# Head shares, evacuations, key requests and the first pair cycle of each feed-forward layer issued in another order

## Chip, cores and metric

One Trainium2 chip, one core used. The metric is the time on the device in microseconds (us) of one launch; lower is better.

## The reference, cut to what matters

Two layers over 576 tokens (512 of a prompt, 64 of a later request that also has 128 cached keys per head), width 1024, all fp32.

```python
def _diff_attend(q_pos, q, k, v, k_pos, rel_table, lam):
    k2 = k.reshape(k.shape[:3] + (2, DIFF_DIM))
    bias = jnp.moveaxis(_rel_bias(k_pos[None, :] - q_pos[:, None], rel_table), -1, 0)
    logits = jnp.einsum('bqhmd,bkhmd->bmhqk', q, k2).astype(jnp.float32) * DIFF_SCALE + bias
    logits = jnp.where(_chunk_mask(q_pos, k_pos), logits, -jnp.inf)
    p = jax.nn.softmax(logits, axis=-1)
    attn = (p[:, 0] - lam * p[:, 1]).astype(v.dtype)
    return jnp.einsum('bhqk,bkhd->bqhd', attn, v)
# even layer: x += concat(latent attention of 8 heads ("mla"),
#                         _rmsnorm(_diff_attend of 8 heads, g_subln)) @ w_out
# odd layer:  x += attention of 8 heads over the 256 keys that an indexer selects ("dsa") @ w_out
# each layer then: h = rmsnorm(x); x += (silu(h @ w_gate) * (h @ w_up)) @ w_down
```

## The kernel before

**Numbers.** Every fp32 operand of a product is split into a high and a low part, and a product is three matmuls: high by high, low by high, high by low. The split of a weight `RAW` is a rounding copy on ScalarE (`WH`, L1892 in attention, L2181 in the feed-forward part) and a subtraction on VectorE (`WL`, L2407, L2860) or on GpSimd (`WL`, L3170).

**Heads.** The 24 heads (0 to 7 mla, 8 to 15 diff, 16 to 23 dsa) run one after another. The function `attention(h)` stands four times, for TensorE (L1531), ScalarE (L2050), VectorE (L2747) and GpSimd (L3256), and each goes through 8 slots `s`. In slots 0 to 4 TensorE makes the scores of token tile `s` (`head_scores`, L1442 and L1418) and transposes the probabilities of the tile before (`turn_probs`, L1455 to L1458). VectorE and ScalarE do the softmax between: mask and maximum L2659, exponent L2016, reciprocal L2667, scaling L2024 in mla and dsa heads; in diff heads the two maps are mixed by `mix_maps` (VectorE L2677). The transposes are split by L2032 (ScalarE) and L2684 (VectorE, `PTl`) before `weighted_values` (L1467) may use them.

**Shares.** A slot also has a share of a later head's projections. `CHUNKS` says which: in mla heads one whole projection (`q`, `k`, `v` and for even heads `pe`, `ps`), in diff and dsa heads a part of q, k and v. A share is a run of 128x288 matmuls of L1206 into one of the two PSUM pairs ACC0 and ACC1, which `group(..., use=LONG or SHORT)` names in `plan_attention`; VectorE reads it out in `write_projection` (`YQ`, `YK`, `YV`; L2585 in diff and dsa heads), and the values are then split in jobs q, k, v: high parts on ScalarE (L1923), low parts on GpSimd (L3177: `Ql`, `Kl`, `Vl`). Odd heads have in slots 0 to 3, even heads in slots 4 to 7, a tile of the output projection of a finished pair of heads (`wo`, L1206 from MIX), added to X by VectorE (L2423).

**Cached keys.** In slot 4 of heads 8 to 14 GpSimd asks for the next head's cached keys (`load_cached_keys`, DMA of KC, L3242) and then does job v; TensorE transposes KC at the end of the head (L1372).

**Norm of a diff head.** Its sums of squares are ten one-column matmuls (`subnorm_sum`, L1214, into ACC1) in slot 3 of the next head. `b_mean` (VectorE L2435, L2436, L2439) reads them out, ScalarE takes the root (L2048), and L1222 spreads the result.

**Feed-forward part.** Its weights run in seven-product cycles over pairs of tiles (`cycle`, L1586 to L1588). The first two tiles, m = 0 and 1 (`PLAIN` = 2), are made one by one with gate and up products (L1206); VectorE copies the up products from PSUM into U (L2985, L2994), ScalarE makes SG (L2189), and GpSimd multiplies (HF, L3320) and splits (HH, L3322) while VectorE prepares the first cycle: sums of token halves (XD, L2896 to L2903), their low parts (TB, L2909), mixed weights (T and S, L2831 to L2847) and the weights' low parts (L2860). ScalarE copies finished products out of PSUM (TC, L2161).

**Order.** Each engine runs its list as it is written out by these functions. Only counted semaphores tie the engines together, so an instruction that waits holds up all behind it on its engine.

## Time and profile before

| | us |
|---|---|
| median of 3 runs | 1730.51 (1728.37 to 1733.53) |
| the profiled execution | 1732.16 |
| its span, first to last instruction | 1730.3 |
| TensorE busy in the span | 1678.6 (97%) |
| VectorE, ScalarE, GpSimd busy | 1114.3, 803.5, 584.6 |
| mean granted TensorE clock | 0.992 of full speed |

The page of the profile gives for each engine its busy time, then the clock in 40 slices, the chain of work that ended last and the costliest groups. Times of rows are microseconds from the start of the span. `[1.45 <-POOL Ql L3177]` behind a row says that the engine had idled 1.45 us before it and that the last thing it waited for was `Ql` of L3177 on GpSimd (POOL). PE is TensorE, DVE VectorE, ACT ScalarE.

### The profile page before, as it was taken

The page shows a single profiled execution, that of the slowest core. Times are in us where ns is not written, and L with a number is a line of the kernel's source. Part 1 is how long each engine was busy: PE and PEld are TensorE (multiplying, and loading weights), DVE is VectorE, ACT ScalarE, POOL GpSimd, SP SyncE. Part 2 cuts the span into 40 slices and gives each one's busy share as a digit, 9 for nine tenths or more (in the row PEclk, how much of TensorE's full clock was granted, in tenths as well). Part 3 has the DMA queues.
Part 4 walks back from the last instruction along what each step waited for, and adds up shares of the span by engine and source line. Part 5 has one row for each costly group of instructions (what it writes and reads, how often), then busy time and mean ns, then how long its engine had stood idle before and what let it go on. Part 6 is the DMA issues. An engine that isn't in the chain of part 4 may idle for free.

```text
span 1730.3 us, 31752 instructions
## 1 busy us (share of the span) xinstructions
PE 1678.6 (97%) x12337; PEld 1617.3 (93%) x12345; DVE 1114.3 (64%) x2086; ACT 803.5 (46%) x1522; POOL 584.6 (34%) x442
## 2 busy tenths in 40 slices
PE   7999999999999999999999999999999999999998
PEld 6889999889898899999999999899989999999998
DVE  4656655555556698478467679633457974884776
ACT  4355555354545555245335445543456551552453
POOL 3344344355443122012102248474451230121122
PEclk9999999999999999999999999999999999999999
DMA  7221132332233123223323242332322332333231
GB/s 195 61 54 56 52 98 68 85 83 73 73 87 91 49 62 110 86 73 98 110 62 100 55 115 69 97 95 78 94 85 67 86 110 62 98 107 89 74 90 64
DMA packets 252104, 145.45 MB, mean 84 GB/s; under 512 B 21934, under 2 KB 242156, under 8 KB 251956
## 3 DMA queue, kind: packets, MB, share of 16 engines
q1 hardware_dynamic: 247080, 135.41, 27.6%
q0 software_dynamic: 4032, 7.77, 1.7%
q8 instruction: 100, 1.64, 0.4%
q14 instruction: 48, 0.39, 0.1%
q10 hardware_dynamic: 844, 0.24, 0.1%
HBM read 130.69 MB, written 15.32 MB: 84 GB/s over the span
## 4 chain that ended last, share of the span: by engine, by line
PE 82%; DVE 10%; ACT 3%; issue 3%; POOL 1%; DMA 1%; SPq 0%; DVEq 0%; ACTq 0%
PE ACC L1206 39%; PE ACC L1586 7%; PE ACC L1588 7%; PE ACC L1587 7%; PE T L1206 3%; PE ACC L1467 2%; PE S L1442 2%; PE S L1206 2%; DVE SCO L2732 2%; DVE TOP L2729 1%; ACT PR L2016 1%; PE S L1588 1%; PE S L1586 1%; PE S L1587 1%; PE S L1418 1%
## 5 line engine op out<-in xcount | busy, mean ns | idle before, releaser
L1206 PE MATMUL ACC<-XGh,WH 128*128 128x288 f32 x1024 | 233.6, 310 | 7.5 <-DVE YK L2585 2.1
L3170 POOL TENSOR_TENSOR WL<-RAW,WH 128x1024 fp32r<-128x1024 f32 (+3 forms) x84 | 180.4, 2150 | 156.9 <-ACT WH L1892 156.7
L3320 POOL TENSOR_TENSOR HF<-SG,U 128x576 f32<-128x576 f32 x44 | 66.6, 1515 | 477.7 <-ACT SG L2189 412.1
L1206 PE MATMUL ACC<-XGh,WL 128*128 128x288 f32 x1024 | 221.0, 298 | 0.0
L1206 PE MATMUL ACC<-XGl,WH 128*128 128x288 f32 x1024 | 220.6, 297 | 0.0
L1586 PE MATMUL ACC<-TB,WH 128*128 128x288 f32 x640 | 189.9, 297 | 5.1 <-DVE WL L2860 4.5
L1892 ACT ACTIVATE WH<-RAW 128x1024 fp32r<-128x1024 f32 (+3 forms) x159 | 153.1, 971 | 81.7 <-PE ACC L1206 43.7
L1588 PE MATMUL ACC<-TB,WL 128*128 128x288 f32 x640 | 189.4, 296 | 0.0
L1587 PE MATMUL ACC<-TB,WH 128*128 128x288 f32 x640 | 189.1, 296 | 0.0
L1206 PE MATMUL ACC<-HH,WH 128*128 128x288 f32 x1032 | 179.3, 295 | 0.0
L1206 PEld LDWEIGHTS ACC<-XGh,WH 128*128 128x128 f32 x1024 | 163.7, 191 | 14.2 <-DVE YK L2585 2.6
L1206 PEld LDWEIGHTS ACC<-XGh,WL 128*128 128x128 f32 x1024 | 165.9, 190 | 0.0
L1206 PEld LDWEIGHTS ACC<-XGl,WH 128*128 128x128 f32 x1024 | 165.8, 190 | 0.0
L1206 PEld LDWEIGHTS ACC<-HH,WH 128*128 128x128 f32 x1032 | 151.3, 188 | 0.0
L2016 ACT ACTIVATE PR<-SX,STAT 128x128 f32<-128x128 f32 (+4 forms) x160 | 85.7, 536 | 131.2 <-DVE STAT L2659 127.6
L1586 PEld LDWEIGHTS ACC<-TB,WH 128*128 128x128 f32 x640 | 120.8, 189 | 6.6 <-DVE WL L2860 4.9
L2423 DVE TENSOR_TENSOR X<-ACC,X 128x576 f32<-128x576 f32 x89 | 66.7, 752 | 89.1 <-PE ACC L1206 85.2
L2407 DVE TENSOR_TENSOR WL<-RAW,WH 128x1024 fp32r<-128x1024 f32 (+2 forms) x75 | 96.3, 1285 | 41.9 <-ACT WH L1892 41.6
L1588 PEld LDWEIGHTS ACC<-TB,WL 128*128 128x128 f32 x640 | 121.1, 189 | 0.0
L1587 PEld LDWEIGHTS ACC<-TB,WH 128*128 128x128 f32 x640 | 121.0, 189 | 0.0
L3322 POOL TENSOR_TENSOR HH<-HF,HH 128x576 fp32r<-128x576 f32 x44 | 67.8, 1541 | 137.6 <-ACT HH L2198 137.6
L1206 PE MATMUL ACC<-HH,WL 128*128 128x288 f32 x516 | 110.1, 294 | 0.0
(459 smaller groups left out, 4342.3 us busy)
## 6 DMA issues: line engine op xcount, KB each, us to landing
RAW<-in_w_gate_dram SPq DMA_DIRECT2D x44, 512.0 KB, 3.9
RAW<-in_w_up_dram SPq DMA_DIRECT2D x44, 512.0 KB, 4.6
RAW<-in_w_down_dram SPq DMA_DIRECT2D x32, 512.0 KB, 4.1
RAW<-in_w_in_even_dram SPq DMA_DIRECT2D x29, 512.0 KB, 5.1
RAW<-in_w_in_odd_dram SPq DMA_DIRECT2D x28, 512.0 KB, 4.4
RAW<-in_w_out_even_dram SPq DMA_DIRECT2D x16, 512.0 KB, 4.2
RAW<-in_w_down_dram SPq DMA_DIRECT2D x16, 384.0 KB, 3.5
RAW<-in_w_out_odd_dram SPq DMA_DIRECT2D x8, 512.0 KB, 5.0
```

The source lines that it names most:

```text
L1206: ins = pe.matmul(out[0:m, 512 * b:512 * b + width], left, right[:, b * width:(b + 1) * width], start=(first and part == 0), stop=(last an ...
L1442: ins = pe.matmul(out[0:r, 0:w], left, right, start=(i == 0), stop=(i == len(products) - 1))
L1586: pe.matmul(out, hi[:, w], xh, start=first and k == 0, stop=False, skip_group_check=not first)
L1587: pe.matmul(out, hi[:, w], xl, start=False, stop=False, skip_group_check=not first)
L1588: ins = pe.matmul(out, lo[:, w], xh, start=False, stop=k == 3, skip_group_check=not first)
L1892: act.activation(WH[slot][:, 0:n], RAW[slot][:, 0:n], ACT.Copy).then_inc(w_hi, 1)
L2016: act.activation(PR[m][0:r, n % 2, 0:w], SX[m][0:r, 0:w], ACT.Exp, bias=STAT[0:r, n % 2, m:m + 1], scale=-1.0, accum_out=STAT[0:r, n % 2, ...
L2407: dve.tensor_tensor(WL[slot][:, 0:n], RAW[slot][:, 0:n], WH[slot][:, 0:n].bitcast(F32), ALU.subtract).then_inc(w_lo, 1)
L2423: return lambda out: dve.tensor_tensor(two(X[:, m, :]), halves(out), two(X[:, m, :]), ALU.add)
L3170: pool.tensor_tensor(WL[slot][:, 0:n], RAW[slot][:, 0:n], WH[slot][:, 0:n].bitcast(F32), ALU.subtract).then_inc(w_lo_pool, 1)
L3320: pool.tensor_tensor(HF[:, q, :], SG[:, q, :], U[:, q, :], ALU.mult).then_inc(h_out, 1)
L3322: pool.tensor_tensor(HH[:, m, 1, :], HF[:, q, :], HH[:, m, 0, :].bitcast(F32), ALU.subtract).then_inc(h_lo, 1)
```

## The change

It moves instructions and changes no arithmetic.

1. **Head 0.** The q share of head 1 (18 matmuls) goes ahead of the first scores, the k share of head 1 writes ACC1, the q share of head 2 moves from head 1's first slot to head 0's slot 5, and ScalarE does job k of head 1 earlier.
2. **Head 6, slot 5.** VectorE's weight split moves behind the evacuations.
3. **Heads 8 to 13, slot 5.** VectorE writes YK before the low parts of the transposes (`keys_early`).
4. **Heads 8 to 14.** GpSimd asks for the cached keys behind job v.
5. **Head 15.** The sums of squares of head 14 go behind the `wo` tile of slot 3; `b_mean` moves from slot 3 to slot 4; one X evacuation of slot 5 moves ahead of PTl, in head 22 too.
6. **Head 16.** A share of 12 matmuls goes ahead of the scores of slot 3; VectorE writes YK one slot later.
7. **First pair cycle of both layers.** ScalarE copies U instead of VectorE. GpSimd's first product waits until VectorE has made the cycle's token sums. VectorE makes the last token sum and the next cycle's weight split ahead of the mix of S4. ScalarE copies t2 and rounds the token sum ahead of S4.

```diff
+def share(h, s):
+    if (h, s) == (0, 5):
+        return 2, "q", 0, QLT, QLT
+    g = prepared_in(h)
+    if g is None or (h, s) == (1, 0):
+        return None
+    c = chunks(g)[s]
+    return c and (g, *c)
+def share_first(h, s):
+    return (h, s) in ((0, 0), (16, 3))
...
+    SHORT_TOO = (("k", 1), ("q", 2), ("q", 18))
@@ TensorE, attention @@
+                    if share_first(h, s):
+                        prepare(*c[:4])
                     if s < TOK_TILES:
                         head_scores(h, s)
...
-                    if s == 3 and h % 16 and kind_of(h - 1) == "diff" and h % 2:
+                    if s == 3 and h in (9, 11, 13):
                         subnorm_sum(h - 1)
...
                     if out_tile(h, s) and (h, s) != (22, 4):
                         output_tile(*out_tile(h, s))
+                    if (h, s) == (15, 3):
+                        subnorm_sum(14)
@@ ScalarE, attention and first cycle @@
+                    if h == 0 and s == 4:
+                        job("k", g)
...
+                    if not before and not part:
+                        seven_copy("t2", layer, part, c)
+                        token_sum_hi(layer, 3, 1)
                     seven_high("S4", layer, part, c)
-                    seven_copy("t2", layer, part, c)
...
+            def take_plain_up(layer, m):
+                act.wait_ge(acc_done, acc.made("u", layer, m))
+                act.wait_ge(acc_free, acc.made("g", layer, m))
+                act.activation(two(U[:, m, :]), halves(pair(acc.at("u", layer, m))), ACT.Copy).then_inc(acc_free, 1)
@@ VectorE, attention @@
-                return s == 5 and (h in (2, 4, 6) or h == 23)
+                return s == 5 and h in (2, 4, 6, 15, 22, 23)
+            def keys_early(h, s):
+                return s == 5 and kind_of(h) == "diff" and prepared_in(h) is not None
...
-                    if s == (3 if h % 2 else 4) and h % 16 and kind_of(h - 1) == "diff":
+                    if s == (3 if h in (9, 11, 13) else 4) and h % 16 and kind_of(h - 1) == "diff":
                         b_mean(h - 1)
...
-                    if h < HEADS and s:
+                    if h < HEADS and s and (h, s) != (6, 5):
                         begin("slot", h, s - 1)
+                    if (h, s) == (6, 6):
+                        begin("slot", h, s - 2)
@@ VectorE, first cycle @@
+                    if not before and not part:
+                        token_sum(layer, 3)
                     mix("S4", layer, part, c)
+                    if not before and not part:
+                        seven_low("WG", layer, part, c + 1)
                     add_up("c11", layer, part, c)
                     seven_low("A22", layer, part, c)
-                    if not before and not part:
-                        token_sum(layer, 3)
...
-                evacuate(("u", layer, 0), lambda out: dve.tensor_copy(two(U[:, 0, :]), halves(out)))
@@ GpSimd @@
-                    if s == 4 and x is not None and kind_of(h) != "mla" and h != 16:
+                    if s == 4 and h > 16 and x is not None:
                         load_cached_keys(x)
                     if s == v_job_slot(h):
                         job("v", h)
...
+                    if s == 4 and x is not None and kind_of(h) == "diff":
+                        load_cached_keys(x)
...
                         pool.wait_ge(sg_done, made)
+                        if m == 0 and not part:
+                            pool.wait_ge(tb_lo, 4 * layer + 4)
```

GpSimd's list in head 8, before and after (WL is a weight's low part, KC the cached keys of head 9, VF its cached values, Ql, Vl and Kl the low parts of the head's q, v and k):

```order
L3177 TENSOR_TENSOR Ql_97<-YQ,Qh_95 128x576
L3170 TENSOR_TENSOR WL_58<-RAW_52,WH_55 128x1024
L3242 DMA KC<-in_cache_diff_k_dram 128x128
L3177 TENSOR_TENSOR Vl<-VF,Vh 128x768
L3170 TENSOR_TENSOR WL_59<-RAW_53,WH_56 128x1024
```

```order
L3229 TENSOR_TENSOR Ql_97<-YQ,Qh_95 128x576
L3222 TENSOR_TENSOR WL_58<-RAW_52,WH_55 128x1024
L3229 TENSOR_TENSOR Vl<-VF,Vh 128x768
L3294 DMA KC<-in_cache_diff_k_dram 128x128
L3222 TENSOR_TENSOR WL_59<-RAW_53,WH_56 128x1024
```

The request for KC stood ahead of Vl and now stands behind it. The same is so in each of the heads 8 to 14; in heads 8, 11 and 13 a WL follows, in the others Kl.

TensorE's list in slots 3 and 4 of head 15, before and after (L1214 and, after, L1237 are the sums of squares of head 14; the runs from MIX are tiles of the output projection, the second of them m = 4):

```order
L1455 MATMUL T<-IDN,PR_81 128x128 x2
L1214 MATMUL ACC<-ONES,SQ 128x1 x4
L1214 MATMUL ACC<-ONES,SQ 64x1
L1206 MATMUL ACC<-MIXh,WH_55 128x288 x2
L1206 MATMUL ACC<-MIXl,WH_55 128x288 x2
```

```order
L1229 MATMUL ACC<-MIXl,WH_55 128x288 x2
L1229 MATMUL ACC<-MIXh,WL_58 128x288 x2
L1237 MATMUL ACC<-ONES,SQ 128x1 x4
L1237 MATMUL ACC<-ONES,SQ 64x1
L1441 MATMUL S<-Kh,Qh_95 64x192 x2
L1441 MATMUL S<-Kl,Qh_95 64x192 x2
L1441 MATMUL S<-Kh,Ql_97 64x192 x2
L1478 MATMUL T<-IDN,PR_81 128x128 x3
L1229 MATMUL ACC<-MIXh,WH_56 128x288 x2
```

The sums, which write ACC1, stood ahead of the twelve matmuls of tile m = 3 (ACC0) and now stand behind them; the next that writes ACC1 is tile m = 4, the last row.

VectorE's list at the end of the first pair cycle's preparations in layer 0, before and after (TB is the low part of a token sum XD; T and S are mixed weights; the G row is a sum of finished products):

```order
L2994 COPY U<-ACC 128x576
L2843 TENSOR_TENSOR S<-RAW_52,RAW_53 128x512
L2909 TENSOR_TENSOR TB<-XD,TB 128x1152
L2860 TENSOR_TENSOR WL_60<-S,WH_57 128x512
L2847 TENSOR_TENSOR S<-RAW_52,T 128x512
L2872 TENSOR_TENSOR G<-S,TC 128x288
L2860 TENSOR_TENSOR WL_63<-RAW_53,WH_62 128x512
L2903 TENSOR_TENSOR XD<-XF,XD 128x1152
L2860 TENSOR_TENSOR WL_58<-RAW_54,WH_55 128x1024
L2909 TENSOR_TENSOR TB<-XD,TB 128x1152
```

```order
L2893 TENSOR_TENSOR S<-RAW_52,RAW_53 128x512
L2959 TENSOR_TENSOR TB<-XD,TB 128x1152
L2910 TENSOR_TENSOR WL_60<-S,WH_57 128x512
L2953 TENSOR_TENSOR XD<-XF,XD 128x1152
L2897 TENSOR_TENSOR S<-RAW_52,T 128x512
L2910 TENSOR_TENSOR WL_58<-RAW_54,WH_55 128x1024
L2922 TENSOR_TENSOR G<-S,TC 128x288
L2910 TENSOR_TENSOR WL_63<-RAW_53,WH_62 128x512
L2959 TENSOR_TENSOR TB<-XD,TB 128x1152
```

The copy of U is gone, the last XD and the next cycle's 1024-column WL (WL_58) stand ahead of the G sum and of WL_63, which were ahead of them.

## Rows read from the trace of the kernel before

**Rows 1.** Windows: length; busy PE, PEld, DVE, ACT, POOL; clock; DMA share; GB/s.

```profile
88.00:95.00 7.00, 7.00 (x32) 6.06 (x31) 3.68 (x7) 1.31 (x4) 1.33 (x2) 0.53 0.42 84
...
308.00:313.00 5.00, 3.59 (x16) 3.48 (x17) 4.03 (x7) 1.84 (x4) 2.72 (x5) 0.66 0.37 105
...
559.00:563.00 4.00, 4.00 (x25) 3.50 (x24) 3.32 (x13) 2.08 (x6) 0.00 (x0) 0.61 0.51 124
...
1358.00:1362.00 4.00, 4.00 (x22) 4.00 (x22) 3.90 (x5) 1.58 (x2) 0.00 (x0) 0.64 0.82 232
```

**Rows 2.** TensorE's timeline, head 0: start, duration, instruction, idle before.

```profile
87.20 0.30 PE L1442 MATMUL S<-Kh,Qh 128*128 128x128 f32 x1 [1.45 <-POOL Ql L3177]
...
105.15 0.21 PE L1457 MATMUL T<-IDN,PR 64*64 64x64 f32 x1 [1.73 <-ACT PR L2024]
```

**Rows 3.** The timeline of GpSimd, VectorE and TensorE, head 8, slot 4.

```profile
303.42 0.56 POOL L3242 DMA_DIRECT2D KC<-in_cache_diff_k_dram  x1
...
305.80 2.35 POOL L3170 TENSOR_TENSOR WL<-RAW,WH 128x1024 fp32r<-128x1024 f32 x1
...
303.62 4.75 DVE L2677 SCALAR_TENSOR_TENSOR PR<-PR,STAT,PR 64x192 f32<-64x192 f32 x1
...
308.52 0.21 PE L1457 MATMUL T<-IDN,PR 64*64 64x64 f32 x1 [2.08 <-DVE PR L2677]
...
309.69 0.85 PE L1206 MATMUL ACC<-XGh,WH 128*128 128x288 f32 x2 [0.89 <-DVE YK L2585]
```

**Rows 4.** The timeline in head 9; last, the keys' DMA by line.

```profile
325.19 4.78 POOL L3170 TENSOR_TENSOR WL<-RAW,WH 128x1024 fp32r<-128x1024 f32 x2 [10.73 <-ACT WH L1892]
...
326.95 0.76 DVE L2677 SCALAR_TENSOR_TENSOR PR<-PR,STAT,PR 128x128 f32<-128x128 f32 x1
...
350.62 1.85 POOL L3177 TENSOR_TENSOR Vl<-VF,Vh 128x768 fp32r<-128x768 f32 x1 [2.91 <-ACT Vh L1923]
...
353.97 0.27 PE L1372 MATMUL T<-IDN,KC 128*128 128x128 f32 x1
...
DMA to landing us min/median/max: 2.2/3.2/4.3
```

**Rows 5.** The timeline of TensorE in slot 5 of head 10.

```profile
382.67 0.53 PE L1206 MATMUL ACC<-XGh,WH 128*128 128x288 f32 x2 [0.39 <-DVE YK L2585]
```

**Rows 6.** The timeline of VectorE and TensorE in head 15.

```profile
559.45 0.14 DVE L2436 TENSOR_SCALAR RS<-ACC 64x1 f32<-64x1 f32 x1
...
562.90 0.16 DVE L2667 RECIPROCAL STAT<-STAT 64x2 f32<-64x2 f32 x1 [0.31 <-ACT PR L2016]
...
561.13 0.83 PE L1206 MATMUL ACC<-MIXh,WH 128*128 128x288 f32 x2
...
568.68 0.49 PE L1222 MATMUL ACC<-IDN,RS 128*128 128x128 f32 x2 [1.21 <-DVE X L2423]
```

**Rows 7.** The timeline, first pair cycle, layer 0; last row layer 1.

```profile
615.54 2.41 POOL L3320 TENSOR_TENSOR HF<-SG,U 128x576 f32<-128x576 f32 x1 [32.42 <-DVE U L2985]
...
616.57 2.46 DVE L2860 TENSOR_TENSOR WL<-RAW,WH 128x1024 fp32r<-128x1024 f32 x1
...
623.55 1.22 DVE L2860 TENSOR_TENSOR WL<-T,WH 128x1024 fp32r<-128x1024 f32 x1
...
624.69 0.75 DVE L2994 COPY U<-ACC 128x576 f32<-128x576 f32 x1
...
630.39 0.41 ACT L2161 ACTIVATE TC<-ACC 128x288 f32<-128x288 f32 x1
...
630.90 0.37 PE L1586 MATMUL ACC<-TB,WH 128*128 128x288 f32 x1 [2.25 <-DVE WL L2860]
...
1357.26 0.42 PE L1586 MATMUL ACC<-TB,WH 128*128 128x288 f32 x1 [2.26 <-DVE WL L2860]
```

**Rows 8.** The timeline of TensorE in heads 7 and 16.

```profile
247.69 0.53 PE L1206 MATMUL ACC<-XGh,WH 128*128 128x288 f32 x2 [0.67 <-DVE X L2423]
...
1096.62 0.46 PE L1442 MATMUL S<-Kh,Qh 128*128 128x512 f32 x1 [2.33 <-DVE SEL L2739]
```

More of the change, by code:

```diff
@@ L420, in plan_pairs @@
             if this:
-                if c + 1 < n:
+                if c + 1 < n and (before or part):
                     add(seven_lo, "WG", c + 1)
@@ L2218, in cycle @@
                     ahead(layer, part, 1, "P5")
-                if c >= 2 and (before or part):
+                if c >= 2 and (part or c > PLAIN + 1):
                     hidden_hi(layer, part, c - 2)
+                if not part and c == PLAIN + 1:
+                    hidden_hi(layer, part, 0)
                 if this:
@@ L2934, in cycle @@
                 if this:
-                    if c + 1 < n:
+                    if c + 1 == n:
+                        begin("ahead", layer, part, 0)
+                    elif before or part:
                         seven_low("WG", layer, part, c + 1)
-                    else:
-                        begin("ahead", layer, part, 0)
                     if not before and not part:
@@ L2993, in ffn @@
                 seven_low("S12", layer, 0, PLAIN)
-                evacuate(("u", layer, 1), lambda out: dve.tensor_copy(two(U[:, 1, :]), halves(out)))
                 mix("S3", layer, 0, PLAIN)
```

67 lines of the change are left out of this document (39 added, 28 removed).

## The prediction

> **What bounds the kernel now.** I read the busy shares first, then the waits of TensorE summed by line, then the timeline around each long one. TensorE is busy 97% of the span, so the time is its matmuls, its idle gaps, and the stretches in which its clock is low. The change leaves every product in place, so all it can move is the gaps and those stretches. In the windows of [rows 1] the granted clock is 0.53, 0.66, 0.61 and 0.64: each holds a stretch at 1.2 GHz instead of 2.4. Such a stretch began in each case right behind a place where TensorE had idled or had run only one-column matmuls. A stretch costs about (1 − clock) × length: (1 − 0.53) × 7.0 = 3.3 us in head 0, 0.34 × 5 = 1.7 in head 8, 0.39 × 4 = 1.6 in head 15, 0.36 × 4 = 1.4 in layer 1's feed-forward part. So a gap costs its length, and sometimes 1.4 to 3.3 us more. VectorE, at 64%, is far from full over the whole, but where TensorE idles it is nearly always a chain through VectorE, and twice VectorE is itself held up beside GpSimd [rows 3, 7].
>
> **Head 0.** TensorE idles 1.45 us for GpSimd's `Ql` before the first scores, and near the head's end 1.73 us for ScalarE's scaling [rows 2]. The 18 matmuls moved ahead need nothing from `Ql`, so the 1.45 goes and with it, I think, the half-clock stretch behind it, 3.3. The share of head 2, taken ahead of the last tile's transposes, lies on the 1.73. Removable: 1.45 + 3.3 + 1.73 = 6.5. But with TensorE earlier, the chain of softmax steps and of head 1's keys (VectorE, ScalarE, then `Kl` on GpSimd) ends last at the head's end, and it gets only part of this. I take 5.0; bounds 1.5 (the first gap alone) and 6.5.
>
> **Heads 6 and 7.** The 0.67 us wait for X [rows 8] goes when the weight split moves behind the evacuations: +0.65, bounds 0.3 and 0.7.
>
> **Head 8.** GpSimd writes the request for KC at 303.42. VectorE asks for its mix at 303.62 and has it only at 308.37, behind `Vl` and behind the WL that ends at 308.15; TensorE idles 2.08, then 0.89 for YK, then runs at half clock, 1.7 [rows 1, 3]. After the change `Vl` (1.85 us, as in [rows 4]) runs at 303.43 to 305.28, the request follows, and VectorE's mix gets in at the boundary, at about 305.4. YK is written before the low parts. Left is some 0.6 us for YK. Gain 2.08 + 0.89 + 1.7 − 0.6 = 4.1; lower bound 0, should the mix stay shut out until the WL ends as it did before; upper bound 4.7.
>
> A rule bears on this term. In the trace the mix stayed out through two instructions of GpSimd, `Vl` and WL [rows 3]. The Trainium skill, page "SBUF — State Buffer", section "Who interferes with whom", says that whichever of VectorE (with two inputs in SBUF) and GpSimd starts first holds the shared ports for its whole instruction, and the other is blocked until then. By that rule the mix should have come in when `Vl` ended, so the row shows a longer block than the rule has. By the rule this term is 4.1, by the row as a precedent it is 0.
>
> I take 4.1 because in head 9 the mix was asked for inside two WLs that run back to back (325.19 to 329.97) and was done in 0.76 us, at the boundary between them [rows 4].
>
> **Head 9.** The request for KC now goes out when `Vl` ends, at 350.62 + 1.85 = 352.47. It lands 2.2 to 4.3 us after issue, median 3.2, so at 354.7 to 356.8, and TensorE transposes KC at 353.97 [rows 4]. That is a new wait of 0.7 to 2.8 us; I take −1.5, and −3.5 at worst with a half-clock stretch behind a long one. In the other heads 8 to 14 the same timeline shows the transposes over 5 us behind `Vl`, more than the longest landing.
>
> **Heads 10, 12 and 14.** TensorE waits 0.39 us for YK in head 10 [rows 5] and likewise in the other two; YK written before the low parts ends that: 3 × 0.39 = +1.2. Lower bound 0. The price, if the mix fails to get in between the WL and `Vl`, is a rival below.
>
> **Head 15.** The wait of 1.21 us for X goes [rows 6], and part of a wait for the squares, 0.3. But the sums' reader moves behind the reciprocal of slot 4, which starts at 562.90; before, it read at 559.45. Tile m = 4, which writes the same bank, was begun at 561.13 [rows 6] and must now wait until about 562.7 (the reciprocal comes a little sooner, the reads take 0.3). TensorE would idle about 2.0 to 2.5 us, where now a half-clock stretch of 1.6 [rows 1] lies, which I expect to stay in another place. Gain 1.21 + 0.3, loss 1.6 to 2.5 less what of it is regained at the next wait: −0.1, bounds −1.7 and +1.0.
>
> **Head 16.** Twelve matmuls fill none of the 2.33 us before the selection is ready, because they stand behind scores that wait for it [rows 8]; they make the slot's scores later and its end less idle. With a possible new half-clock stretch, +0.2, bounds −1.2 and +1.0.
>
> **Feed-forward part, layer 0.** TensorE idles 2.25 us at 630.90. The row names a WL, but the bank is freed by ScalarE's copy of t2, begun at 630.39, behind a rounding that waits for VectorE's mix [rows 7]. VectorE gets there late: the WL at 616.57 takes 2.46 us against 1.22 for the same shape at 623.55, because GpSimd's HF began before it; two copies of U cost 2 × 0.75 [rows 7]; a token sum's low part is also about 1.2 us longer beside GpSimd. After the change 1.2 + 1.2 + 1.5 = 3.9 us leave VectorE, and t2 is copied ahead of the rounding. Against that ScalarE copies U behind a rounding, which gives the second up product its bank about 0.5 us later. The gap of 2.25 goes, and with it hardly more, since TensorE has no other long gap there: +2.2, bounds 1.0 and 3.0. What is late next is VectorE's weight split for the following cycle, which the change moves ahead.
>
> **Feed-forward part, layer 1.** The same gap, 2.26 [rows 7], and here the half-clock stretch follows, 1.4 [rows 1]: +3.6, bounds 1.5 and 4.8. GpSimd's held products cost nothing: the next user of their buffers is the gate of tile 2, a whole cycle later.
>
> **Sum.** 5.0 + 0.65 + 4.1 − 1.5 + 1.2 − 0.1 + 0.2 + 2.2 + 3.6 = 15.35. The profiled execution took 1732.16 us, so 1716.8 on its scale. The median of the runs is 1.65 lower, 1730.51, which gives 1715.2. I take 1716.
>
> **Rivals.**
> *The gaps are only partly cured.* Where TensorE comes earlier, it next meets the softmax chain, the keys of head 9 and the bank in head 15, each at its worse bound, and head 0 gives 2.5 instead of 5: 1716 + 2.5 + 2.0 + 1.6 = 1722. For it: all these chains run through the same two engines. Against: the gaps before and after are of different lengths, and the chains have slack at most of them. Chance 0.14.
> *The mix stays shut out for one instruction.* In heads 10, 12 and 14 `Vl` now begins straight behind WL, where the request used to stand between. If GpSimd goes on without letting VectorE in, the mix is late by `Vl`'s 1.85 us, 3 × (1.85 + 0.39), and head 8 gives half: 1716 + 6.7 + 2 = 1725. For it: the block in head 8; against: the mix in head 9. Chance 0.09.
> *Slower: shut out as in head 8.* If every mix asked for beside back-to-back work of GpSimd is held until that work ends, each of the five heads 10 to 14 costs what head 8 cost, 2.08 + 0.89 + 1.7 = 4.7. Head 8 and heads 10, 12 and 14 lose their gains, 4.1 and 1.2: 1716 + 5 × 4.7 + 5.3 = 1745. It decides from the point where GpSimd's next instruction is taken before VectorE's waiting one in at least four of the five. Against it: [rows 4]. Chance 0.04.
> *It doesn't do what it says.* The gaps are there for another reason (the clock drops whatever stands before the scores of head 0, t2's copy is late for another wait), and the gains are eaten: 1729. Chance 0.04.
> The forecast has the remaining 0.69.
>
> **Range and chances.** From the bounds of the unknown costs, the worse ends that may fall together (head 0 at 1.5, head 8 at 0) give 1716 + 3.5 + 4.1 = 1723.6, and the first two rivals reach to 1725; I close at 1726. The better ends (head 0 6.5, both feed-forward parts, head 15 +1.0, head 9 −0.7) sum to 1716 − 1.5 − 2.0 − 1.1 − 0.8 = 1710.6, and what overlaps the half-clock stretches leave open is some 2 us more: 1708. A measurement of this kernel can tell about 0.3%, 5.2 us, from no change: faster means below 1725.3. Faster 0.86, within 0.10, slower 0.04.
>
> **What would show it.** Head 0: no idle before L1442's first scores and a clock near 1 there. Head 8: VectorE's mix done by 306 instead of 308.4, and the clock of 308 to 313 near 1. Head 9: a wait of TensorE for the DMA of KC of 1 to 2 us. Head 15: a wait of tile m = 4 for RS of 2 us or more. Both feed-forward parts: the wait before the seventh product gone, HF begun only after the fourth token sum, and the 1024-column WL at 1.2 us. The prediction is wrong if the mixes of heads 10, 12 and 14 take over 3 us, if gaps gone in one place stand a few us further on with their length, or if new half-clock stretches appear behind the new waits.

## The result

| | median, us | runs | ratio to the kernel before, 95% interval |
|---|---|---|---|
| before | 1729.68 | 4 (1728.37 to 1733.53) | |
| changed | 1715.65 | 4 (1713.06 to 1716.73) | 0.9912 (0.9895 to 0.9929) |

The change makes the kernel 0.9% faster. The profiled execution of the changed kernel took 1716.73 us, its span is 1714.6 (before 1732.16 and 1730.3). The forecast was 1716, in a range of 1708 to 1726. So the total came out, but as will be seen two of its terms were wrong, others made up for them, and 0.69 us of the traced difference arose before any part of the change.

**Where the time went.** TensorE makes the same 12337 matmuls in both kernels, nearly in the same order. So the n-th matmul of one trace can be laid beside the n-th of the other, and the difference of their start times, read at places that no part of the change moves, gives the gain up to that place. The step between two such places is the gain of the stage between them. Each trace is one execution: over the twelve other traces of the experiments below and of a repeat, a step whose instructions are the changed kernel's came out again within 0.06 us in head 0, 0.02 in head 8, some 0.3 in each feed-forward part, but 1.4 to 1.5 in heads 15 and 16. The first step, in which nothing was changed, lies between -0.66 and -1.95 over all of them, so it varies by 1.3 us with the same instructions and is not shown to come from the change.

| stage (read at, us of before) | difference after it | step | forecast |
|---|---|---|---|
| start (59.9) | -0.69 | -0.69 | |
| head 0 (150.0) | -6.28 | -5.59 | -5.0 |
| heads 6 and 7 (260.0) | -7.13 | -0.85 | -0.65 |
| head 8 (329.9) | -11.64 | -4.51 | -4.1 |
| head 9 (370.1) | -10.87 | +0.77 | +1.5 |
| heads 10 to 14 (550.0) | -12.34 | -1.47 | -1.2 |
| head 15 and the end of the layer's attention (592.0) | -11.04 | +1.30 | +0.1 |
| feed-forward part, layer 0 (700.0) | -13.61 | -2.57 | -2.2 |
| up to head 16 (1080.1) | -13.80 | -0.19 | |
| head 16 (1199.9) | -12.59 | +1.21 | -0.2 |
| feed-forward part, layer 1 (1400.1) | -15.68 | -3.09 | -3.6 |
| last matmul (1722.9) | -15.70 | -0.02 | |

The table of windows of the changed kernel (length; busy time and count of PE, PEld, DVE, ACT, POOL; TensorE's granted clock; DMA share; GB/s) covers the places of [rows 1]:

```profile
80.00:90.00 10.00, 9.74 (x70) 8.39 (x69) 6.09 (x13) 4.98 (x9) 2.92 (x2) 1.00 0.07 13
...
296.00:302.00 6.00, 6.00 (x47) 5.77 (x46) 5.61 (x8) 3.31 (x7) 5.98 (x5) 1.00 0.36 98
...
550.00:554.00 4.00, 3.48 (x15) 3.46 (x16) 0.81 (x5) 3.63 (x5) 2.72 (x2) 0.57 0.00 0
...
1090.00:1096.00 6.00, 5.55 (x23) 5.27 (x24) 2.10 (x8) 2.65 (x6) 5.02 (x8) 0.50 0.25 61
...
1343.00:1347.00 4.00, 4.00 (x33) 4.00 (x32) 4.00 (x6) 0.44 (x2) 1.43 (x1) 1.00 0.87 251
```

Head 0 is the first of these rows, head 8 the second, then head 15, head 16 and layer 1's first pair cycle. The clock is 1.00 in head 0, head 8 and layer 1's first pair cycle, where it was 0.53, 0.66 and 0.64. In head 15 it is as low as before, and head 16 has 0.50.

The timeline of TensorE (start, duration, instruction, idle time before it and what ended that) shows both gaps of [rows 2] gone, only one wait of 0.84 us being left, then the last transposes and the v share of head 8 without the waits of [rows 3], the new wait of head 9, and the new wait of head 15:

```profile
98.50 0.63 PE L1478 MATMUL T<-IDN,PR 128*128 128x128 f32 x4 [0.84 <-ACT PR L2051]
...
299.25 0.24 PE L1480 MATMUL T<-IDN,PR 64*64 64x64 f32 x1
...
299.48 0.53 PE L1229 MATMUL ACC<-XGh,WH 128*128 128x288 f32 x2
...
343.04 0.30 PE L1395 MATMUL T<-IDN,KC 128*128 128x128 f32 x1 [0.56 <-DMA KC<-in_cache_diff_k_dram]
...
550.52 0.85 PE L1229 MATMUL ACC<-MIXh,WH 128*128 128x288 f32 x2 [2.95 <-DVE RS L2478]
```

In head 8 GpSimd now begins Vl before it writes the request for the keys, and VectorE's mix, asked for inside Vl, ends with it (296.48 + 1.88 = 298.36; Vl ends at 298.15). In head 10 the mix gets in between WL and Vl (367.67 + 1.12 = 368.79; the WL ends at 368.58), as the row of head 9 in [rows 4] had it:

```profile
296.30 1.85 POOL L3229 TENSOR_TENSOR Vl<-VF,Vh 128x768 fp32r<-128x768 f32 x1
...
296.48 1.88 DVE L2719 SCALAR_TENSOR_TENSOR PR<-PR,STAT,PR 64x192 f32<-64x192 f32 x1
...
368.54 1.93 POOL L3229 TENSOR_TENSOR Vl<-VF,Vh 128x768 fp32r<-128x768 f32 x1
...
367.67 1.12 DVE L2719 SCALAR_TENSOR_TENSOR PR<-PR,STAT,PR 64x192 f32<-64x192 f32 x1
```

In layer 0's first pair cycle ScalarE copies t2 from 616.05 to 616.46, 1 us before the seventh product begins at 617.44, VectorE's split of the next cycle's weight takes 1.22 us and ends at 618.0, 1.0 us before its matmul of 619.03, and GpSimd's first product comes at 620.37, behind all of this. TensorE has no gap there, where [rows 7] had 2.25 us:

```profile
616.05 0.41 ACT L2190 ACTIVATE TC<-ACC 128x288 f32<-128x288 f32 x1 [0.47 <-PE ACC L1615]
...
616.78 1.22 DVE L2910 TENSOR_TENSOR WL<-RAW,WH 128x1024 fp32r<-128x1024 f32 x1
...
620.37 1.43 POOL L3377 TENSOR_TENSOR HF<-SG,U 128x576 f32<-128x576 f32 x1 [48.31 <-DVE TB L2959]
```

### The profile page after: what moved, and what is told of

The parts are those of the page before. It is cut to its first block, busy times and chain, and to the rows that moved or that the text cites. A ratio compares the mean times of both kernels' runs of the same rounds, so it can differ in the third digit from the quotient of the medians.

```text
span 1714.6 us, 31759 instructions
## 1 busy us (share of the span) xinstructions
PE 1672.7 (98%) x12337; PEld 1612.3 (94%) x12345; DVE 1107.5 (65%) x2082; ACT 805.2 (47%) x1526; POOL 581.1 (34%) x442
## 3 DMA queue, kind: packets, MB, share of 16 engines
q8 instruction: 100, 1.64, 0.4%
## 4 chain that ended last, share of the span: by engine, by line
PE 81%; DVE 11%; ACT 4%; issue 2%; POOL 1%; DMA 1%; ACTq 0%; DVEq 0%
PE ACC L1229 40%; PE ACC L1613 7%; PE ACC L1615 7%; PE ACC L1614 7%; PE T L1229 3%; PE ACC L1490 2%; PE S L1229 2%; PE S L1465 2%; DVE SCO L2774 2%; ACT PR L2043 1%; DVE TOP L2771 1%; PE S L1615 1%; PE S L1613 1%; PE S L1614 1%; PE T L1478 1%
```

## The experiments

Each kernel below is the changed kernel with the edit shown, and the traces are compared by the table's method. The theory was that of the prediction: a gap of TensorE costs its length and sometimes a stretch at 1.2 GHz behind it, and the gaps come from late chains, twice through a collision of VectorE and GpSimd. Its rivals stand with each run. Each of the ten experiments was run once, and single times of one kernel differ by some 3 us, so what is read from them is the trace.

### Head 0: which of the two moves

```diff
 def share_first(h, s):
-    return (h, s) in ((0, 0), (16, 3))
+    return (h, s) == (16, 3)
```

> The changed kernel with one thing undone: in head 0 the scores of tile 0 come before the q share of head 1 again. Theory (the idle time starts the half-clock stretch): TensorE idles 1.4 us for Ql before the first scores again, the clock then is at half for some 7 us (a window of 7 us behind it shows 0.5 to 0.6), and against the changed kernel TensorE is 1.4 + 3.3 = 4.7 us late by the k and v share, of which up to 1 us is taken back at the next wait for probabilities: 3.5 to 4.7 us in all. Rival (the slow stretch came from the small transposes there, not from the gap): 1.4 us and the clock stays near 1.

The time was 1718.83 us. The wait for Ql is back to the hundredth, with a slow stretch behind it:

```profile
86.00 0.30 PE L1465 MATMUL S<-Kh,Qh 128*128 128x128 f32 x1 [1.45 <-POOL Ql L3229]
...
88.00:95.00 7.00, 7.00 (x42) 7.00 (x41) 3.70 (x10) 2.30 (x6) 1.50 (x1) 0.76 0.40 84
```

The gap gives 1.45 and the clock (1 - 0.76) x 7 = 1.7. Behind them TensorE is 2.9 us later than in the changed kernel, and 0.7 of these are regained at a later wait for probabilities; head 0's step is -3.35 instead of -5.59, so the share costs 2.2 us where it stood before. That the slow stretch belongs to the scores placed first, with their wait, is shown: it is there in the two traces that have this order, and none of the twelve others has one in head 0. Its price isn't fixed: 1.7 us here, 3.3 in the kernel before [rows 1] for the same 1.45 us of idle time. The expectation, 3.5 to 4.7, was too high by this.

```diff
 def share(h, s):
-    if (h, s) == (0, 5):
-        return 2, "q", 0, QLT, QLT
     g = prepared_in(h)
-    if g is None or (h, s) == (1, 0):
+    if g is None:
...
-    SHORT_TOO = (("k", 1), ("q", 2), ("q", 18))
+    SHORT_TOO = (("k", 1), ("q", 18))
```

> The changed kernel with the q share of head 2 back in the first slot of head 1. Theory: TensorE meets the wait for ScalarE's probabilities of the last tile again, 1.7 us, and the wait for Kl behind it, 0.3: 1.5 to 2.1 us later from head 1 on than in the changed kernel. Rival (the chain through job k sets the time whatever fills it): under 0.5 us.

The time was 1716.44 us. The wait for the last tile's probabilities is back and no slow stretch came with it:

```profile
99.50 0.21 PE L1478 MATMUL T<-IDN,PR 64*64 64x64 f32 x1 [1.57 <-ACT PR L2049]
```

Head 0's step is -4.12 instead of -5.59: 1.5 us, as the theory had it, and the rival (the chain through job k sets the time) is out.

### Head 8: what blocked VectorE

```diff
-                    if s == 4 and h > 16 and x is not None:
+                    if s == 4 and x is not None and (h > 16 or h in (8, 9, 10, 11, 12, 13, 14)):
                         load_cached_keys(x)
                     if s == v_job_slot(h):
                         job("v", h)
...
-                    if s == 4 and x is not None and kind_of(h) == "diff":
-                        load_cached_keys(x)
```

> The changed kernel with the request for the cached keys ahead of job v in heads 8 to 14 again; YK stays early. Theory (the order on GpSimd made the block): in head 8 VectorE's mix takes 4 to 5 us again, TensorE idles about 2 us before the last transposes and runs 3.4 us at half clock, about 4 us later in all; in head 9 the wait for KC, 0.6, goes: 3.4 us later from head 9 on. Rival (YK ahead of the low parts was the cure): under 1 us. The gains of heads 10, 12 and 14 (0.4 to 0.5 each) stay by either.

The time was 1716.99 us.

```profile
295.62 0.56 POOL L3294 DMA_DIRECT2D KC<-in_cache_diff_k_dram  x1
296.20 1.85 POOL L3229 TENSOR_TENSOR Vl<-VF,Vh 128x768 fp32r<-128x768 f32 x1
298.01 2.35 POOL L3222 TENSOR_TENSOR WL<-RAW,WH 128x1024 fp32r<-128x1024 f32 x1
...
295.82 4.76 DVE L2719 SCALAR_TENSOR_TENSOR PR<-PR,STAT,PR 64x192 f32<-64x192 f32 x1
...
300.72 0.21 PE L1480 MATMUL T<-IDN,PR 64*64 64x64 f32 x1 [2.08 <-DVE PR L2719]
...
301.30 0.53 PE L1229 MATMUL ACC<-XGh,WH 128*128 128x288 f32 x2 [0.30 <-DVE YK L2627]
...
301.00:305.00 4.00, 3.70 (x28) 3.70 (x29) 3.17 (x6) 1.86 (x4) 2.95 (x4) 1.00 0.52 144
```

The block of [rows 3] is back: 4.76 us, with VectorE asking 0.20 us after the request began, as before, and TensorE's 2.08 us. The rival is out. The second wait is 0.30 instead of 0.89, which is what the early YK gives, and this time the clock stays at 1.00. So head 8's 4.5 us (its step is -2.07 here) are made up of 2.4 for the order on GpSimd, 0.6 for the early YK, and the rest, some 1.5, for a slow stretch that followed the two waits together in the kernel before and doesn't follow the longer one here. Whether the early YK or chance took it away isn't shown. The expected loss of about 4 us was too high by that stretch. Head 9 is 0.8 us better (its step -0.04 instead of +0.77), so over both heads the new place of the request brings 1.6 us.

Is it the order on GpSimd itself? Two more kernels ask. The first puts the request behind the second WL, so that in head 8 WL, Vl and WL run back to back:

```diff
-                    if s == 4 and x is not None and kind_of(h) == "diff":
+                    if s == 4 and x is not None and kind_of(h) == "diff" and h != 8:
                         load_cached_keys(x)
...
                     begin("slot", h, s)
+                    if (h, s) == (8, 4):
+                        load_cached_keys(x)
```

> The changed kernel with the request for the cached keys of head 9 one place later still, so that in head 8 GpSimd runs WL, Vl, WL back to back and then writes the request. It separates two causes of the block in head 8. If the request between two products lets the second one in ahead of VectorE (cause A), the mix, asked for during Vl, is done when Vl ends, in 1.9 us, as in the changed kernel, and nothing is lost. If any back-to-back pair on GpSimd keeps VectorE out (cause B), the mix is held until the second WL ends, takes 4 us or more, and TensorE idles 1.5 to 2 us, with half clock 3 to 4 us later in all. Cause A is likelier, 0.75.

The time was 1715.64 us.

```profile
295.88 1.85 POOL L3229 TENSOR_TENSOR Vl<-VF,Vh 128x768 fp32r<-128x768 f32 x1
297.68 2.52 POOL L3222 TENSOR_TENSOR WL<-RAW,WH 128x1024 fp32r<-128x1024 f32 x1
...
296.05 1.88 DVE L2719 SCALAR_TENSOR_TENSOR PR<-PR,STAT,PR 64x192 f32<-64x192 f32 x1
```

The mix was asked for inside Vl, a WL followed at once, and VectorE still got in when Vl ended, at 297.73 + 0.20. Cause B is out: work back to back on GpSimd doesn't keep VectorE out. Head 8's step is -4.51, as in the changed kernel. The same trace has a third meeting of this kind: a VectorE instruction, a weight's split with both inputs in SBUF, is asked for while GpSimd writes a request (300.15 to 300.71), 0.21 us before the product `Kl` (300.73 to 302.17). It too was held through the product behind the request, 2.75 us instead of 1.22; here no second product followed at once:

```profile
300.52 2.75 DVE L2449 TENSOR_TENSOR WL<-RAW,WH 128x1024 fp32r<-128x1024 f32 x1 [0.39 <-ACT WH L1919]
```

A product close behind did not do it without a request. In heads 11, 13 and 15 of the kernel before the same mix was asked for 0.16 to 0.28 us before `Vl` began, with no request under way, and took 0.40 us each time; in head 11, where `Vl` began at 420.84:

```profile
420.56 0.40 DVE L2677 SCALAR_TENSOR_TENSOR PR<-PR,STAT,PR 64x192 f32<-64x192 f32 x1
```

The second kernel puts the request ahead of job v in heads 8 to 14 again, by the edit of the first run of this section, and moves VectorE's mix ahead of an X evacuation, in head 8 alone:

```diff
                         mix_maps(h, s - 1)
+                    if (h, s) == (8, 5):
+                        evacuate(("wo", *out_tile(8, 4)), add_to_x(out_tile(8, 4)[1]))
...
-                    if out_tile(h, s) and not out_early(h, s):
+                    if out_tile(h, s) and not out_early(h, s) and (h, s) != (8, 4):
```

> GpSimd's list as in the kernel before (the request for the cached keys ahead of job v in heads 8 to 14), the rest as in the changed kernel, and in head 8 one thing on VectorE: the mix of the last tile stands ahead of the X evacuation of slot 4, so it is asked for some 0.8 us earlier, inside GpSimd's WL and not while GpSimd writes the request. Theory (the order on GpSimd is not enough for the block, the mix must be asked for during the request): the mix is done when the WL ends, it takes 1 to 2 us instead of 4.76, and TensorE's wait of 2.08 us is gone with GpSimd's old order; the X evacuation comes 0 to 1 us later. Rival (the request ahead of Vl makes GpSimd go on through Vl and WL whenever VectorE asks): the mix is held until the second WL ends, over 4 us, and TensorE waits 2 us or more.

The time was 1716.10 us.

```profile
293.88 2.40 POOL L3224 TENSOR_TENSOR WL<-RAW,WH 128x1024 fp32r<-128x1024 f32 x1
296.20 0.56 POOL L3296 DMA_DIRECT2D KC<-in_cache_diff_k_dram  x1
...
295.33 1.17 DVE L2719 SCALAR_TENSOR_TENSOR PR<-PR,STAT,PR 64x192 f32<-64x192 f32 x1 [0.35 <-ACT PR L2051]
...
299.18 0.24 PE L1480 MATMUL T<-IDN,PR 64*64 64x64 f32 x1
```

With the old order on GpSimd the mix takes 1.17 us and TensorE doesn't wait. The kernel before shows the same in heads 10, 12 and 14, where GpSimd's list is WL, request, `Vl` and the mix is asked for inside the WL: 1.11 to 1.12 us. So the order on GpSimd is not the cause by itself: the block of 4.76 us comes where VectorE asks while GpSimd writes a request and a product follows 0.38 us later. Either engine's order cures it, and this one leaves head 9 without a wait: the steps are -4.51 and -0.05, 0.8 us better than the change's own way. Why such a mix then stays out through two products, when one asked for inside a product waits for one alone, stays open; two traces show it, and no run varied the moment within the request.

### Head 15: the sums of squares and their reader

```diff
-                    if s == 3 and h in (9, 11, 13):
+                    if s == 3 and h in (9, 11, 13, 15):
                         subnorm_sum(h - 1)
...
-                    if (h, s) == (15, 3):
-                        subnorm_sum(14)
...
-                    if s == (3 if h in (9, 11, 13) else 4) and h % 16 and kind_of(h - 1) == "diff":
+                    if s == (3 if h % 2 else 4) and h % 16 and kind_of(h - 1) == "diff":
                         b_mean(h - 1)
```

> The changed kernel with head 14's sums of squares ahead of the output tile of slot 3 in head 15 again and their reader in slot 3; the early X evacuation of slot 5 stays. Theory (the reader behind the reciprocal of slot 4 costs a wait of 2.95 us and a half-clock stretch): both go, a wait for the squares of 0.4 to 0.7 us and a half-clock stretch of 3.4 us come back in slot 3: 2.6 us earlier than the changed kernel from the end of head 15 on. Rival (the softmax chain of tile 4 ends last there anyway): TensorE meets the wait at the next transposes and the gain is under 1 us.

The time was 1712.98 us. TensorE waits for the squares again, and no longer for their reader:

```profile
544.13 1.23 PE L1235 MATMUL ACC<-ONES,SQ 128*128 128x1 f32 x10 [0.66 <-ACT SQ L2065]
...
570.00:576.00 6.00, 6.00 (x47) 6.00 (x46) 4.92 (x7) 4.31 (x7) 0.13 (x1) 1.00 0.00 0
```

The stage's step is -2.19 instead of +1.30, 3.5 us better. 1.9 of these are there from 556 on, 1.5 come from the window 570 to 576, whose clock is 1.00 here and 0.72 in the changed kernel, though nothing differs there but the moment at which TensorE comes. The changed kernel's own code in this stage has steps of +0.99 to +1.38 in six traces and +1.94 to +2.43 in five, by how long the clock is low, while TensorE's idle time in it, added up, is 5.3 to 5.4 us in all eleven. It is 3.4 here and 3.9 in the kernel before. So this part of the change, the reader's move above all, is a loss of 1.9 us of idle time. Of the early X evacuation, kept here, these traces show a gain of 0.4 us; the rest of the -2.19 is that one slow stretch of the kernel before is missing, and nothing shows that the evacuation took it away.

### Head 16: the share ahead of the scores

```diff
 def share_first(h, s):
-    return (h, s) in ((0, 0), (16, 3))
+    return (h, s) == (0, 0)
...
-                    if h == 16 and s == 4:
+                    if h == 16 and s == 3:
                         write_projection(g, "k")
```

> The changed kernel with head 16 as before: scores of slot 3 first, YK written in slot 3. Theory (twelve matmuls ahead of the scores only move the idle time behind them, where it comes in pieces and keeps the clock down twice as long): the wait for the selection grows from 0.7 to 2.3 us, the waits of 0.88, 1.10 and 0.85 us behind it shrink to one of 1.1, the half-clock stretch shrinks from 6.8 to 3.4 us: 1.6 us earlier than the changed kernel. Rival (the loss of 1.6 us in the changed kernel's head 16 comes from elsewhere, for instance from an earlier arrival): within 0.5 us.

The time was 1717.18 us, and the theory fell. The idle times are as it said, and yet the stage is no faster: its step is +1.61, where the changed kernel had +1.21, and not 1.6 us better as expected.

```profile
1082.95 0.77 PE L1465 MATMUL S<-Kh,Qh 128*128 128x512 f32 x1 [2.31 <-DVE SEL L2781]
...
1091.80 0.33 PE L1395 MATMUL T<-IDN,KC 128*128 128x128 f32 x1 [1.15 <-DVE PTl L2726]
...
1082.00:1086.00 4.00, 3.05 (x9) 2.39 (x11) 2.04 (x10) 2.62 (x5) 1.83 (x2) 0.59 0.23 55
...
1094.00:1098.00 4.00, 4.00 (x24) 3.94 (x24) 0.46 (x4) 1.84 (x4) 3.00 (x2) 0.70 0.10 29
```

These are the instructions and the waits of the kernel before (2.31 and 1.15 us; before 2.33 and 1.13), but with two slow stretches where the kernel before had one, after each wait: (1 - 0.59) x 4 + (1 - 0.70) x 4 = 2.8 us. What differed between before and changed here was the clock. The changed kernel's own code shows it too. The windows of three executions of that same head:

```profile
1090.00:1098.00 8.00, 7.55 (x37) 7.21 (x38) 2.73 (x11) 2.76 (x7) 6.71 (x8) 0.59 0.19 46
...
1090.00:1098.00 8.00, 7.29 (x34) 6.88 (x35) 2.54 (x10) 2.92 (x8) 6.99 (x8) 0.57 0.20 46
...
1090.00:1098.00 8.00, 6.21 (x36) 5.81 (x37) 3.95 (x13) 4.27 (x11) 7.03 (x9) 0.79 0.18 46
```

The first two are the changed kernel, in its two profiled executions, the third is the kernel with the requests ahead of job v again, whose head 16 has the same instructions. The clock is 0.59, 0.57 and 0.79, and the steps of the stage are +1.21, +1.48 and +0.06. Over the eleven traces with this head 16 the step lies at -0.01 to +0.46 in five and at +1.10 to +1.48 in six. So the stage's loss is not the work of the moved share. Nor does the share bring a gain that these traces can show: the old order has +1.61 here and +1.63 in the last kernel below, but 0 in the kernel before, where one slow stretch stands in this head and not two. TensorE's idle time in the stage, added up, is 4.1 us in these three traces and 4.0 to 4.2 in the eleven with the share.

### The first pair cycle: which of three parts

First without GpSimd's wait, and with ScalarE's roundings of its products where they had been:

```diff
-                        if m == 0 and not part:
-                            pool.wait_ge(tb_lo, 4 * layer + 4)
...
-                if c >= 2 and (part or c > PLAIN + 1):
+                if c >= 2 and (before or part):
                     hidden_hi(layer, part, c - 2)
...
                 gate(layer, 0, 1, (acc_free, acc.made("g", layer, 1)))
+                hidden_hi(layer, 0, 0)
                 seven_high("S12", layer, 0, PLAIN)
```

> The changed kernel with GpSimd's first two hidden products not held back in the first pair cycle, and ScalarE's roundings of them where they were. Theory 1 (the hold is what cures the gap): VectorE's weight split beside HF and a token sum's low part beside HF or HH take 1.2 us longer each, and TensorE idles 1 to 2 us before the seventh or the next product in both layers. Theory 2 (the other order and the copies of U on ScalarE suffice, VectorE then has 1 us of slack): TensorE idles under 0.7 us there. I hold 1 at 0.4, 2 at 0.6.

The time was 1717.49 us.

```profile
613.58 1.88 POOL L3371 TENSOR_TENSOR HF<-SG,U 128x576 f32<-128x576 f32 x1
...
614.08 2.59 DVE L2956 TENSOR_TENSOR TB<-XD,TB 128x1152 fp32r<-128x1152 f32 x1
...
620.33 0.40 PE L1613 MATMUL ACC<-XGh,WH 128*128 128x288 f32 x1 [0.54 <-DVE WL L2907]
...
622.66 0.38 PE L1613 MATMUL ACC<-TB,WH 128*128 128x288 f32 x1 [0.48 <-DVE TB L2956]
```

The low parts of two token sums take 2.40 us (at 606.58) and 2.59 us instead of 1.36 beside HF (the second beside the one at 613.58), and TensorE idles 0.54 and 0.48 us. The steps of the two feed-forward stages are -1.88 and -2.25 instead of -2.57 and -3.09: the hold is worth 0.7 and 0.8 us. In the ten traces whose first pair cycle is the changed kernel's the two steps lie at -2.35 to -2.69 and -3.06 to -3.35, so such differences are good to some 0.3 us. The gap of 2.25 us is not back, so the hold is not what cures it; but the waits, 1.0 us in all, are more than the 0.7 of theory 2.

Then with U copied by VectorE (the two `take_plain_up` calls out, the two `evacuate(("u", ...), tensor_copy)` in again):

> The changed kernel with the two copies of U on VectorE again. VectorE gets 2 x 0.75 us more ahead of the seventh product, 0.6 of which its idle time there takes: the weight split for the next cycle comes 0.9 us later, where it had 1.0 us to spare. If this account of the slack is right, TensorE idles 0 to 0.3 us and the time is that of the changed kernel. If the copies were what made the gap, 1 us or more comes back in each layer.

The time was 1717.85 us. TensorE waits in each layer, later than I had placed it, for a token sum's low part, and 0.38 us more behind that for a copy of U; in layer 0:

```profile
620.74 0.37 PE L1613 MATMUL ACC<-TB,WH 128*128 128x288 f32 x1 [0.48 <-DVE TB L2957]
```

The steps are -1.77 and -2.46: 0.8 and 0.6 us for the copies. The slack of 1.0 us before the split held; the low part behind it had none.

Last with both engines' order as before, the hold and ScalarE's copies of U kept:

```diff
-                    if not before and not part:
-                        token_sum(layer, 3)
                     mix("S4", layer, part, c)
-                    if not before and not part:
-                        seven_low("WG", layer, part, c + 1)
                     add_up("c11", layer, part, c)
                     seven_low("A22", layer, part, c)
+                    if not before and not part:
+                        token_sum(layer, 3)
...
-                    if not before and not part:
-                        seven_copy("t2", layer, part, c)
-                        token_sum_hi(layer, 3, 1)
                     seven_high("S4", layer, part, c)
-                    if before or part:
-                        seven_copy("t2", layer, part, c)
+                    seven_copy("t2", layer, part, c)
+                    if not before and not part:
+                        token_sum_hi(layer, 3, 1)
```

> The changed kernel with the order of the first pair cycle as before (on VectorE the mix of S4, the sum and the half weight's split ahead of the last token sum and the next cycle's split; on ScalarE the copy of t2 behind the rounding of S4), while GpSimd is still held back and ScalarE still copies U. If VectorE being late was the whole cause, the mix of S4 is ready at once and the seventh product waits under 0.2 us; the next cycle's split then comes about 0.9 us after its matmul wants it: TensorE idles 0.5 to 1.0 us in each layer, 1 to 2 us in all. If the order of ScalarE's copy was the cause, the gap of 2 us is back before the seventh product.

The time was 1716.10 us. No wait comes back before the seventh product in either layer; what comes back is a wait for U, 0.31 us in layer 0 (at 624.00) and in layer 1

```profile
1348.58 0.40 PE L1611 MATMUL ACC<-XGh,WH 128*128 128x288 f32 x1 [0.32 <-DVE U L2926]
```

The steps are -2.15 and -2.75: the order is worth 0.4 and 0.3 us, which is little more than such differences are good to. So the gap of 2.25 us came from VectorE being late, and not from the order in which ScalarE copied; the two parts that take work and collisions off VectorE cure it together. Any two of the three parts cure it, as the three runs show; none with one part alone was run.

### A version with three moves taken back or put otherwise

It has the request for the keys behind job v in head 8 alone, head 16 as before, and in head 15 the reader of the sums at the end of slot 3:

```diff
+                    if s == 4 and x is not None and (h > 16 or h in (9, 10, 11, 12, 13, 14)):
+                        load_cached_keys(x)
                     if s == v_job_slot(h):
                         job("v", h)
...
+                    if s == 4 and h in (8,):
+                        load_cached_keys(x)
...
                         evacuate(("wo", *out_tile(h, s)), add_to_x(out_tile(h, s)[1]))
+                    if (h, s) == (15, 3):
+                        b_mean(14)
```

> The changed kernel with three things taken back or put otherwise: the cached keys are asked for behind job v in head 8 alone; head 16 is as before; in head 15 the sums stay behind the output tile of slot 3, but their reader comes at the end of slot 3, right behind that tile's evacuation. Expected against the changed kernel: 0.6 us in head 9, 1.6 us in head 16, and in head 15 the wait of 2.95 us shrinks to about 0.5 and the half-clock stretch goes, 2.5 to 4 us: 4.7 to 6.2 us earlier, so a ratio to the kernel before of 0.988 to 0.989 where the changed kernel has 0.991. If the waits only move, it is within 2 us of the changed kernel.

> The changed kernel as it is, for the comparison with the version above on one chip: 0.991 of the kernel before.

| five rounds on one chip | median, us | ratio to the kernel before, 95% interval |
|---|---|---|
| before | 1730.70 (9 runs) | |
| changed | 1715.80 (5 runs) | 0.9915 (0.9898 to 0.9931) |
| the version | 1712.12 (4 runs) | 0.9892 (0.9876 to 0.9908) |

Its runs (1710.40 to 1713.46) all lie below those of the changed kernel (1714.78 to 1717.62) on that chip, though the intervals of the two ratios overlap, and one run of the changed kernel in the first comparison took 1713.06. The difference is 3.7 us, where 4.7 to 6.2 had been expected: what is missing is the 1.6 us of head 16. TensorE's waits in head 15 are 0.39 us for the sums and 0.55 for X behind them:

```profile
546.80 0.54 PE L1229 MATMUL ACC<-MIXh,WH 128*128 128x288 f32 x2 [0.39 <-DVE RS L2478]
...
555.02 0.53 PE L1229 MATMUL ACC<-MIXh,WH 128*128 128x288 f32 x2 [0.55 <-DVE X L2465]
```

The steps: head 9 +0.01 instead of +0.77, head 15 -1.64 instead of +1.30, head 16 +1.63 instead of +1.21. The gain is that of heads 9 and 15, and of head 15's 2.9 us 1.7 are a slow stretch less. Taking the share of head 16 back brought nothing that the traces show. A version with that share ahead, or with the mix moved in head 8 instead of the request, was not run.

## Why the prediction was right, and where it wasn't

**The frame held.** The work is the same, and gaps and slow stretches are all that changed. The steps above sum to 15.70 us, the forecast's terms to 15.35; the steps for which the forecast has a term sum to 14.80, and 0.69 of the rest is the start.

**Head 0**, 5.6 against 5.0: both moves cure their own gap, and the doubt that the chain through the keys would take much of it back was too large. The two undone alone cost 2.2 and 1.5, 3.7 together; the rest, 1.9, is nearly all the slow stretch, 3.3 us before and 1.7 when the gap was put back.

**Heads 6 to 8 and 10 to 14**, 6.8 against 5.95: each step is within 0.5 us of its term. The mix got in between WL and Vl, so the rivals that had it shut out in heads 10 to 14 are out. In head 8 the 0.6 us that I left for YK were not there. But the reason was half right: I took the order on GpSimd for the cause, and the block needs the moment at which VectorE asks as well, inside the request.

Here the Trainium skill, page "SBUF — State Buffer", section "Who interferes with whom" (the one that starts first has the shared ports for its instruction, the other is blocked until then), agrees with the mixes asked for inside a product: 1.88 us in head 8 with 1.67 of Vl left, 1.12 in head 10, 1.17 with the mix moved. It doesn't describe the mix asked for during a request, 4.75 and 4.76 us through two products. The prediction overlooked that this mix was asked for 0.38 us before `Vl` began [rows 3]: by whoever starts first, it would not have waited for `Vl` either.

**Head 9**, -0.8 against -1.5, within its bounds. The step that failed is the landing: the request went out at 340.75 and TensorE's wait ended at 343.04, 2.3 us later, near the shortest landing of [rows 4] and not the median that I took.

**Head 15**, -1.3 against -0.1, inside its bounds of -1.7 and +1.0. The term was mis-sized: the wait for the reader was 2.95 us and not 2.0 to 2.5. TensorE was ready for the tile at 547.57, 1.2 us sooner than at 561.13 before, and the reciprocal came only 0.7 sooner (549.82 against 562.90), both after the 12.34 us are taken off by which the whole stage is earlier. I expected some of it back at the next wait, and nothing came back beyond the gains that the term has. The slow stretch behind it cost 1.7 us ((1 - 0.57) x 4), as the one that it replaced did, so the stage's loss here is idle time: 5.3 us, added up, against 3.9 before. In five traces of that same code this stage came out 0.6 to 1.1 us worse still, at -1.94 to -2.43, below the term's lower bound of -1.7.

**Head 16**, -1.2 against +0.2, at its lower bound. My sentence that the twelve matmuls fill none of the 2.33 us was wrong: they stand ahead of the scores that wait for the selection, and the wait fell to 0.71 us. The idle time came back behind it, in waits of 0.88, 1.10 and 0.85 us:

```profile
1082.80 0.47 PE L1465 MATMUL S<-Kh,Qh 128*128 128x512 f32 x1 [0.71 <-DVE SEL L2781]
...
1087.59 0.63 PE L1478 MATMUL T<-IDN,PR 128*128 128x128 f32 x4 [0.88 <-ACT PR L2051]
...
1089.32 0.21 PE L1480 MATMUL T<-IDN,PR 64*64 64x64 f32 x1 [1.10 <-ACT PR L2051]
...
1090.45 0.47 PE L1395 MATMUL T<-IDN,KC 128*128 128x128 f32 x1 [0.85 <-DVE PTl L2726]
```

The loss in this trace is the clock's, a second slow stretch of 1.7 us, and in five of eleven traces of that same head the stage loses under 0.5 us. The idle time of the stage hardly changed, so a gain of 0.2 is not shown either.

**Feed-forward parts**, 5.7 against 5.8: the account by VectorE's lateness was right. The new order of VectorE and ScalarE, on which I counted for t2 and for the next split, is worth 0.3 to 0.4 us. And I missed that the low part behind the weight's split has no slack.

The forecast of 1716 was thus met with head 0, head 8 and head 9 some 1.7 us better than their terms, and heads 15 and 16 some 2.6 worse. That these cancel to within a microsecond is luck, and so are the low-clock stretches of heads 15 and 16, which another execution has longer or shorter by 1.7 us. The first rival, waits that only move, is what happened in heads 15 and 16.

## What to carry to other kernels

Lay the matmuls of two traces side by side by their number: each stage then shows its own gain, to 0.1 us where the clock stays high and to 0.3 in the feed-forward parts here, where whole runs of 1715 us differ by 3. Before a step is credited or blamed for a difference, look at the clock of that stage in several executions, since a slow stretch that costs 1.7 us comes and goes with the same instructions; the idle time of a stage, added up, was steadier. And a reader moved behind a late instruction must be costed by who needs its bank next: here it took 2.95 us, more than the wait of 0.66 us for the squares that it was to save.

## What was not expected of the hardware

A VectorE instruction with two inputs in SBUF (the mix) asked for while GpSimd writes a DMA request, 0.38 us before a product starts, was shut out for 4.75 us, through that product and the next; asked for inside a product it waited for that product alone. It happened in both traces in which the two met like this, and was gone when either engine's order moved. A VectorE split asked for during a request in a third trace was held through the one product that followed. Nearer to a boundary something like it shows in the changed kernel: VectorE's split at 300.95, asked for 0.14 us before a WL of GpSimd ends and 0.09 before Kl begins, takes 2.61 us instead of 1.22, and so waits for Kl as well. Ten of the other traces have the same meeting, with 2.58 to 2.64 us:

```profile
298.68 2.41 POOL L3222 TENSOR_TENSOR WL<-RAW,WH 128x1024 fp32r<-128x1024 f32 x1
301.04 1.43 POOL L3229 TENSOR_TENSOR Kl<-YK,Kh 128x576 fp32r<-128x576 f32 x1
...
300.95 2.61 DVE L2449 TENSOR_TENSOR WL<-RAW,WH 128x1024 fp32r<-128x1024 f32 x1 [0.39 <-ACT WH L1919]
```

And a gap doesn't fix what it costs in clock. The same wait of 1.45 us was followed by 3.3 us lost at the lower clock in one kernel and 1.7 in another, the 2.08 us of head 8 by 1.7 (with 0.89 us more behind it) and by none, and head 16 with its instructions unchanged by about 1.7 or about 3.4.
